# RWKV sample update moved into the inversion levels on 128 partitions, gate tiles put between the recurrence steps, HGRN level operations merged from 16 to 4

## The reference, cut to what matters

```python
# RWKV-7: matrix state per head, 64x64, for prompt (chunked in the kernel) and for the 8 sample rows
sa = jnp.einsum("bhvk,bhk->bhv", s, -kk_t)
s = (s * w_t[:, :, None, :] + sa[..., None] * (kk_t * a_t)[:, :, None, :]
     + v_t[..., None] * k_t[:, :, None, :])
o = jnp.einsum("bhvk,bhk->bhv", s, r_t)
...
# merge of the three branches, z_g is part of the input projection (3 * 1024 columns)
gates = jax.nn.sigmoid(z_g).reshape(B, T, N_BRANCHES, D_MODEL)
merged = gates[:, :, 0] * y_rwkv + gates[:, :, 1] * y_hgrn + gates[:, :, 2] * y_sgu
```

## Time and profile before

| what | value |
|---|---|
| time, median of 3 runs (lowest, highest) | 3241.63 us (3241.45, 3241.85) |
| the profiled execution's own time | 3241.09 us |
| its span, first to last instruction | 3239.3 us |
| PE busy, share of the span | 2957.5 us, 91% |
| DVE busy | 1832.0 us, 57% |
| ACT busy | 1071.3 us, 33% |
| POOL busy | 524.2 us, 16% |

### The profile page before, as it was taken

One profiled execution on the slowest core, in us unless ns is written; L12 is line 12 of the kernel. 1 busy time (PEld: TensorE's weight loads), 2 busy tenths in 40 slices (PEclk: granted clock), 3 DMA queues, 4 the chain that ended last, 5 costly groups with the idle time before them and its releaser, 6 DMA issues.

```text
span 3239.3 us, 54519 instructions
## 1 busy us (share of the span) xinstructions
PE 2957.5 (91%) x20890; PEld 2722.8 (84%) x20890; DVE 1832.0 (57%) x2953; ACT 1071.3 (33%) x1744; POOL 524.2 (16%) x220
## 2 busy tenths in 40 slices
PE   7897867989999999999998978589899999999998
PEld 5687655878899999999976866558789999999997
DVE  1742585217956676666627317752199466666665
ACT  1211121004543334555502112200155443355554
POOL 0000010005862220000000000200078522300000
PEclk9996776999999999999998958769999999999999
DMA  5210310333553335555451103113245433355553
GB/s 188 79 66 27 109 65 30 130 117 109 158 160 120 122 119 162 180 181 179 156 185 66 66 14 114 60 43 143 91 137 162 150 123 122 118 174 177 181 181 123
DMA packets 113036, 395.78 MB, mean 122 GB/s; under 512 B 17122, under 2 KB 18658, under 8 KB 111780
## 3 DMA queue, kind: packets, MB, share of 16 engines
q1 hardware_dynamic: 105124, 379.18, 35.7%
q10 hardware_dynamic: 7808, 15.21, 1.6%
HBM read 385.44 MB, written 8.53 MB: 122 GB/s over the span
## 4 chain that ended last, share of the span: by engine, by line
PE 60%; issue 21%; POOL 8%; DVE 8%; ACT 1%; DMA 0%; ACTq 0%; POOLq 0%; SPq 0%; DVEq 0%
PE bank L414 59%; POOL WHL L1679 7%; DVE arena L1171 5%; POOL arena L1675 1%; ACT arena L872 1%; DVE arena L1269 0%; PE bank L565 0%; DMA arena<-arena 0%; DVE hT L1179 0%; ACT L872 0%; DVE arena L1353 0%; DVE arena L1360 0%; PE bank L607 0%; DVE arena L1175 0%; ACTq L966 0%
## 5 line engine op out<-in xcount | busy, mean ns | idle before, releaser
L414 PE MATMUL bank<-HHL,WHL 128*128 128x264 f32 x6144 | 796.4, 288 | 26.8 <-POOL WHL L1679 21.2
L414 PEld LDWEIGHTS bank<-HHL,WHL 128*128 128x128 f32 x6144 | 763.8, 190 | 37.3 <-POOL WHL L1679 28.4
L414 PE MATMUL bank<-AHL,WHL 128*128 128x264 f32 x6144 | 747.9, 284 | 0.0
L414 PEld LDWEIGHTS bank<-AHL,WHL 128*128 128x128 f32 x6144 | 747.7, 188 | 0.0
L872 ACT ACTIVATE WHL<-raw 128x1024 fp32r<-128x1024 f32 x512 | 542.4, 1060 | 335.3 <-PE bank L414 333.7
L1679 POOL TENSOR_TENSOR WHL<-raw,WHL 128x1024 fp32r<-128x1024 f32 x188 | 485.2, 2587 | 1006.0 <-ACT WHL L872 1006.0
L414 PE MATMUL bank<-hT,ring 128*128 128x264 f32 (+1 forms) x2496 | 588.6, 397 | 19.6 <-DVE hT L1179 11.7
L414 PEld LDWEIGHTS bank<-hT,ring 128*128 128x128 f32 x2496 | 481.6, 194 | 114.8 <-DVE hT L1179 12.5
L414 PE MATMUL bank<-arena 64*64 64x64 f32 (+7 forms) x3200 | 352.7, 280 | 123.0 <-DVE arena L1171 112.6
L414 PEld LDWEIGHTS bank<-arena 64*64 64x64 f32 (+3 forms) x3200 | 319.5, 187 | 164.8 <-DVE arena L1171 108.1
L1171 DVE TENSOR_TENSOR arena<-arena 128x128 f32<-128x128 f32 (+5 forms) x422 | 289.2, 727 | 227.4 <-ACT arena L872 145.6
(11 more groups left out here) (108 smaller groups left out, 1485.2 us busy)
## 6 DMA issues: line engine op xcount, KB each, us to landing
raw<-down SPq DMA_DIRECT2D x256, 512.0 KB, 3.5
raw<-up SPq DMA_DIRECT2D x256, 512.0 KB, 3.5
ring<-wm SPq DMA_DIRECT2D x100, 1024.0 KB, 4.9
arena<-hs ACTq DMA_DIRECT2D x2, 1280.0 KB, 7.7
o_hs<-arena ACTq DMA_DIRECT2D x2, 1280.0 KB, 4.5
arena<-cm SPq DMA_DIRECT2D x2, 1160.0 KB
arena<-rs ACTq DMA_DIRECT2D x2, 1024.0 KB, 7.6
o_rs<-arena ACTq DMA_DIRECT2D x2, 1024.0 KB, 6.8
```

What stands on the lines that cost most here:

```text
L414: return pe.matmul(out, lhsT, rhs, start=start, stop=stop)
```

## The change

It consists of three parts.

First, the sample update. Its transposes stand on PE right after the matmuls of the inversion's setup, the six copies and twelve transfers (two halves each) on ACT before the inversion levels. The layout is 128 partitions: 64 as before, times two halves of the value index. The state arrives by SP (two transfers, after seven ring loads). The nine DVE operations are now 128x2048 (the reductions too) and stand in three parts of three, behind the last addition of levels 2, 3 and 4. ACT sends the result away after the inversion. The arena grows by 4096 columns for it.

Second, the gate tiles. Tiles 0 to 17, in two blocks before, are placed one by one: tile 0 before the token transposes; in each recurrence step half a tile behind y, its other half behind u, a whole tile behind s (tiles 1 to 8); tile 9 behind the recurrence; 10, 11 and 12 around the group norm; half a tile behind each of HGRN levels 0 to 5 (13 to 15); one behind each of the two HGRN state steps (16, 17). Tiles 13 to 17 are copied by ACT without sigmoid, and one sigmoid over all five comes later.

Third, each HGRN level has its subtractions and multiplications over all four heads in one instruction per half: 2 + 2 instead of 8 + 8.

```diff
+                pe.wait_ge(S["mat_evac"], l * 8 + 6)
+                for g in range(6):
+                    if g >= 2:
+                        pe.wait_ge(S["sq_evac"], l * 6 + g - 1)
+                    for j in range(NW):
+                        ins = pe.transpose(bank[g % 2][0:DEC, j * P:(j + 1) * P], SQ[:, g, j, :], ident)
+                    ins.then_inc(S["sq_mm"], 1)
                 pe.wait_ge(S["l_evac"], l * 2 + 1)
...
+                def gate_part(n, out, first, end):
+
+                    slot = (19 + n // 2) % RINGP
+                    if first == 0:
+                        if n % 2 == 0:
+                            arrive(slot, l)
+                        pe.wait_ge(S["gate_evac"], l * 24 + n + 1)
+                    for k in range(first, end):
+                        ins = mm(out[:, 0:T], ring[:, 2 * slot + n % 2, k, :], hT[:, k, 0:T], k == 0, k == KD - 1)
...
+                gate_part(0, bank[2], 0, KD)
                 pe.wait_ge(S["x_done"], l + 1)
...
                     ins.then_inc(S["y_mm"], 1)
+                    gate_part(1 + 2 * n, bank[3], 0, 4)
                     pe.wait_ge(S["y_evac"], e)
...
                     ins.then_inc(S["u_mm"], 1)
+                    gate_part(1 + 2 * n, bank[3], 4, KD)
                     pe.wait_ge(S["u_evac"], e)
...
                     ins.then_inc(S["s_mm"], 1)
-
-                pe.wait_ge(S["o_evac"], (l + 1) * NRC)
-                for g in range(6):
...
+                    gate_part(2 + 2 * n, bank[2], 0, KD)
...
-                for n in range(12):
-                    gate_tile(n, (19 + n // 2) % RINGP, bank[2 + n % 2])
...
+                gate_part(9, bank[3], 0, KD)
+                pe.wait_ge(S["so_in"], 32 * (l + 1))
...
                 spread(YR, bank[2:6], bones).then_inc(S["gn_sq"], 1)
+                gate_part(10, bank[6], 0, KD)
...
+                    if lev < 6:
+                        n = 13 + lev // 2
+                        gate_part(n, bank[6 + n % 2], 4 * (lev % 2), 4 * (lev % 2) + 4)
...
                     ins.then_inc(S["hs_mm"], 1)
+                    pe.wait_ge(S["gate_evac"], l * 24 + 18 + c)
+                    gate_part(16 + c, bank[7], 0, KD)
...
+                for g in range(6):
+                    act.wait_ge(S["sq_evac"], l * 6 + g + 1)
+                    src = TQ[g // 3][0:DEC, g % 3]
+                    for half in range(2):
+                        hp = slice(64 * half, 64 * half + 64)
+                        if g < 5:
+                            act.dma_start(RQ[hp, g], src).then_inc(S["rq_in"], 16)
...
+                act.wait_ge(S["gate_evac"], l * 24 + 20)
+                late = GEA[:, 10:15, :]
+                f(late, late, ACT.Sigmoid).then_inc(S["late_gates"], 1)
...
+                def sample_state(part):
+
+                    if part == 0:
+                        dve.wait_ge(S["sr_in"], 32 * (l + 1))
+                        dve.wait_ge(S["rq_in"], 192 * (l + 1))
+                        step(tt(TR, SR, nkk, ALU.mult))
+                        step(dve.tensor_reduce(SA, TR, AX.X, ALU.add))
+                        step(tt(SR, SR, w, ALU.mult))
+                    elif part == 1:
+                        step(tt(TR, over(SA, RN), kka, ALU.mult))
+                        step(tt(SR, SR, TR, ALU.add))
+                        step(tt(TR, over(VQ2, RN), k2, ALU.mult))
+                    else:
+                        step(tt(SR, SR, TR, ALU.add))
+                        step(tt(TR, SR, r, ALU.mult))
+                        done(dve.tensor_reduce(OS, TR, AX.X, ALU.add), "sr_done", l + 1)
...
+                    if 2 <= lev < LEV_R - 1:
+                        sample_state(lev - 2)
...
-                step(tt(T64, S64, rows(nkk, RN), ALU.mult))
...
+                    halves = [x[:, :, 0:SEQ].rearrange("p j (n b) -> p j n b", b=2 * b)
+                              for x in (BC, hx, HG[:, 4:8, :], HG[:, 0:4, :])]
+                    bc, hh, kk_, qq = halves
+                    ref = bc[:, :, :, b - 1:b].broadcast_to([P, NW, SEQ // (2 * b), b])
+                    tt(hh[:, :, :, 0:b], ref, bc[:, :, :, 0:b], ALU.subtract)
+                    ins = tt(hh[:, :, :, b:2 * b], bc[:, :, :, b:2 * b], ref, ALU.subtract)
...
+                    tt(hh[:, :, :, 0:b], hh[:, :, :, 0:b], kk_[:, :, :, 0:b], ALU.mult)
+                    ins = tt(hh[:, :, :, b:2 * b], hh[:, :, :, b:2 * b], qq[:, :, :, b:2 * b], ALU.mult)
```

More of the change, by code:

```diff
@@ L931, in _ @@
                 z_out(22, 25)
+                for g in range(6):
+                    act.wait_ge(S["sq_mm"], l * 6 + g + 1)
+                    f(TQ[g // 3][0:DEC, g % 3], bank[g % 2][0:DEC, :], ACT.Copy).then_inc(S["sq_evac"], 1)
+                for g in range(6):
+                    act.wait_ge(S["sq_evac"], l * 6 + g + 1)
+                    src = TQ[g // 3][0:DEC, g % 3]
+                    for half in range(2):
+                        hp = slice(64 * half, 64 * half + 64)
+                        if g < 5:
+                            act.dma_start(RQ[hp, g], src).then_inc(S["rq_in"], 16)
+                        else:
+                            part = src.rearrange("b (h c v) -> b h c v", h=RH, c=2)[:, :, half, :]
+                            act.dma_start(VQ2[hp], part).then_inc(S["rq_in"], 16)
                 z_out(25, 26, 4)
@@ L942, in _, with gate_sigmoid @@
                         z_out(26 + 3 * (lev - 1), 29 + 3 * (lev - 1), 4)
+                act.wait_ge(S["sr_done"], l + 1)
+                for half in range(2):
+                    hp = slice(64 * half, 64 * half + 64)
+                    part = OT[0:DEC].rearrange("b (h c v) -> b h c v", h=RH, c=2)[:, :, half, :]
+                    act.dma_start(part, OS[hp]).then_inc(S["so_in"], 16)
+                    act.dma_start(d["o_rs"][l][:, half * VH:(half + 1) * VH, :], SR[hp]).then_inc(S["sr_out"], 16)
+                def gate_sigmoid(e, src, fn=ACT.Sigmoid):
+                    act.wait_ge(S["gate_mm"], l * 24 + e + 1)
+                    f(early_gate(e), src[:, 0:T], fn).then_inc(S["gate_evac"], 1)
+                gate_sigmoid(0, bank[2])
                 for n in range(NRC):
@@ L984, in _ @@
                 f(HV["QH"], HG[:, 12:16, :], ACT.Sigmoid).then_inc(S["hg_sig"], 1)
-                for e in range(12, 16):
-                    act.wait_ge(S["gate_mm"], l * 24 + e + 1)
-                    f(early_gate(e), bank[e % 2][:, 0:T], ACT.Sigmoid).then_inc(S["gate_evac"], 1)
+                for e in range(10, 13):
+                    gate_sigmoid(e, bank[6 + e % 2])
                 act.wait_ge(S["hg_in"], l + 1)
@@ L994, in _ @@
                 f(HV["KH"], HV["U2"], ACT.Ln).then_inc(S["f_ln"], 1)
-                for e in range(16, 18):
-                    act.wait_ge(S["gate_mm"], l * 24 + e + 1)
-                    f(early_gate(e), bank[e % 2][:, 0:T], ACT.Sigmoid).then_inc(S["gate_evac"], 1)
                 act.wait_ge(S["b_ready"], l + 1)
@@ L1016, in _ @@
                       ACT.Copy).then_inc(S["ho_evac"], 1)
+                    gate_sigmoid(16 + c, bank[7], ACT.Copy)
                 act.wait_ge(S["hs_evac"], l * 3 + 3)
```

117 lines of the change are left out of this document (47 added, 70 removed).

## The result

The changed kernel takes 3104.87 us (median; 3104.42 to 3106.68), the kernel before 3241.74 in the same comparison: ratio 0.9577, 95% interval 0.9565 to 0.9589. The profiled execution took 3104.68 us. The forecast was 3129 us with a range from 3108: right in sign and in its main mechanism, 24 us too slow, and 3 us outside the range. The largest part of what is missing, almost half, is in one term, the HGRN levels.

A forecast was written before the change was run, and what follows sets the result against it. PE's order, in turn with DVE's chains, bounds the kernel, with PE's waits lowering its clock. Per layer 56.4 + 5.4 - 4.9 - 1.0 = 55.9, both 111.8; 3241.1 - 111.8 = 3129.3 us, range 3108 to 3158.

The forecast's parts named there:

- The recurrence: Inversion's end to first group norm sum: gate tiles fill PE's waits, full clock, 14.0 us a step; gain 56.4 a layer.
- rival 1: Gate and recurrence work: clock stays at 1.2 GHz throughout, 15 us a layer slower, 3271 us; chance 0.04.
- rival 2: Recurrence: clock falls for about half of it, taking half of 56.4 us a layer, 3186 us; chance 0.10.
- rival 5: Gate tiles wait for their weights at the ring, so the change does nothing that counts; chance 0.02.
- rival 3: HGRN levels gain nothing, or transfers or sample parts slow the inversion; each 3139 to 3140 us; chance 0.17.
- The levels: HGRN level 0 to level 7: DVE and POOL set the pace, 6.4 us a level; gain 5.4 a layer, bounds 0 and 13.
- second reading: HGRN levels: only POOL's addition after the second mask costs DVE anything, 1.1 us, making a level 5.2 us.
- rival 4: HGRN levels: POOL holds DVE less, 7 us a layer more gain, 3115 us; chance 0.11.
- The clock in the levels: HGRN levels: low clock costs PE 7.4 us a level; if it rises, under 4, and DVE and POOL set the pace.
- Ahead of the inversion: Sample transposes before the inversion outlast PE's 3.97 us hole by 1.4; net loss 1.0 a layer, bounds -1 and +2.
- Tile 0 and the token transposes: Behind the inversion: gate tile 0 takes 5.6 us, covering a 2.57 us DVE wait; transposes and copies then 7.2.
- State steps: HGRN state steps: two gate tiles of 3.65 us put in, covering 2.4 us of waits; loss 4.9 a layer.

The follow-up runs named there:

- matmuls of no use: Kernel before with 16 useless matmuls added to each recurrence step, behind y, u and s, nothing removed: 3226.84 us, ratio 0.9953.
- block behind the recurrence: Changed kernel with gate tiles 1 to 8 taken out of the recurrence and put in one block behind it: 3174.05 us.
- four kernels: Changed kernel with 16 operations a level 3123.07 us, without half tiles in the levels 3127.47, without POOL's additions 3092.79; kernel before with merged operations only 3237.53.
- thinner transposes: Changed kernel with one matmul instead of four in each of six groups of sample transposes before the inversion: 3117.95 us.
- unmerged: Changed kernel with the HGRN level operations unmerged again, 16 a level instead of 4, half tiles kept in the levels: 3123.07 us.
- no additions: Changed kernel without POOL's 14 additions a layer in the HGRN levels, all waits kept: 3092.79 us.
- half of the columns: Changed kernel with matmuls, masks and POOL's additions of HGRN levels 1 to 7 on the non-zero half of the columns: 3096.73 us.

## Why the prediction came out as it did

- *The recurrence* was right: full clock, a step of 14.09 us against 14.0 forecast, no idle piece. The matmuls of no use show that filling does it, the block behind the recurrence that nothing else in the change does. Rivals 1, 2 and 5 are out, and rival 3 too, as the levels gain and the inversion is no longer than before.
- *The levels* are the step that failed: 11.1 us instead of 5.4 a layer, almost half of what is missing. The cost that was wrong is POOL's: the sum of 6.2 us a level, and the 6.4 taken, charged both of POOL's additions to DVE in full, 2 x 1.37. Measured is 4 operations at 3.79, two masks of 0.69, and 0.35 of gaps: 5.51. The additions cost 1.29, not 2.74; the sum was off by less, 0.7, because it also left out one mask of 0.69 and the gaps. It is nearly the second reading (5.2; 1.1 for the additions), rival 4, to which I gave 0.11 because one operation of 1351 ns stood still for a whole addition. But a level has two additions, and in that stretch of the trace the other fifteen operations took 277 to 291 ns: only that one was held. The other addition (452.01 to 453.27) lay beside a wait of DVE and a mask and cost nothing, and I did not read it so. The Trainium skill ("SBUF — State Buffer", section "Who interferes with whom") says that a VectorE instruction with two SBUF inputs and a GpSimd instruction that reads SBUF block each other fully. The runs agree that the operations wait (2.50 alone, 3.79 beside POOL) and the masks, which read PSUM, do not (0.69 with and without POOL); the 6.2 was my sum, not the rule.
- *The clock in the levels* was only a condition in the forecast ("If it rises, PE needs under 4"). The four kernels show that it is worth 1.3 us a level, as much as the additions.
- *Ahead of the inversion* the net loss of 1.0 was a gain of 2.0. The bound on that side was 1. I charged 1.4 us for transposes that outlast the hole, from 3.58 us for 16 of a layer's 24 records (the 48 of the prediction are those of both layers). That row was at the lower clock; in their new place all 24 take 3.6 us (157.43 to 161.06), at a clock of 1.00, and end within the hole. What the tile might win was left open: it took 3.93 us, and the end of the inversion was faster too; with thinner transposes the tile is back at 5.62.
- *Tile 0 and the token transposes* took 10.7 us, 12.8 forecast. I kept 7.2 for transposes and copies; at the full clock the transposes are 3.80, and then ACT's copies end it, 5.6 in all. With tile 0 moved away they are 5.55 again.
- *State steps*: a loss of 3.15 instead of 4.9. In the steps themselves it is 3.9 (12.7 us for 8.8); 0.8 is won between level 7 and them, where no tile was put. The first step's matmuls are faster (2.94 for 3.49), but they stand ahead of the tile; without tiles they took 3.72 in one run and 3.00 in another. What made them faster stays open.
- *The sample operations* cost nothing, as forecast (20.1 us for nine are 2.2 each, as the sum had it).

So four terms were off in one direction, with one cause behind two of them, those ahead of the recurrence: I counted the better clock where I had put it to use, in the recurrence, and not for the short pieces of unchanged work around it. The range ended at 3108 because it took rival 4 "less a few us" and did not let it meet a gain in the other terms.

## What to carry to other kernels

Where PE waits often and shortly, work that is needed anyway is worth most between those waits, since it raises the clock for the pieces between them as well (y 3.86 to 2.16 us); count that for the neighbours too. Work behind a wait can be cold (the z tile took 5.62 us behind 3.97 us of waiting and 3.93 behind the transposes), so a piece put ahead of a short stage can pay by itself, but two tiles of 3.7 us in the state steps, whose waits are 1.67 and 0.69 us, cost more than they cover. When two parts of a change act on one loop that passes through two engines, cost them together: merging gained 0.6, filling 0.7, both 1.9.

## What was not expected of the hardware

- Matmuls whose result nobody reads made a kernel faster by 15 us of 3242.
- The clock can alternate in a loop whose turns are alike: in the unmerged kernel the same 16 records took 3.53, 2.05, 3.66 and 2.05 us in four levels.
- The same code behind the same wait does not warm up alike in every run. The 16 records that start the second layer took 5.51 us in the changed kernel's profile and 6.67 in that with tile 0 moved, after the same 4.04 us of waiting. Level 0 of the first layer began between 374.47 and 377.22 us in the changed kernel and in three others that change nothing ahead of it (unmerged, no additions, half of the columns), so single profiles were compared by the length of a step or a level, and whole times by their medians. Why the warming differs stays open.
